# The end of a two-block network kernel: the last 256 output channels with tokens on the partitions

## The chip, the cores and the metric

The kernel runs on one core of a Trainium2 chip. The metric is the device time of one execution in microseconds, from the launch of the program to its end on the chip; the table below gives the median of three runs. A profile of one further execution gives a time for each instruction.

## What is computed

The reference runs two network blocks over 1024 tokens with 1024 channels each (attention, a state-space branch and a feed-forward part in the first; three gated branches in the second). Only the very end of the second block matters here:

```
merged = (jax.nn.sigmoid(g_a) * y_a + jax.nn.sigmoid(g_b) * y_b
          + jax.nn.sigmoid(g_c) * y_c)
return x + merged @ w_o
...
return _rmsnorm_2(x, final_g)      # x / sqrt(mean(x*x) + eps) * final_g, per token
```

`merged` is 1024 tokens by 1024 channels, `w_o` is 1024 by 1024. The mean of the norm runs over all channels of a token, so no output row can be scaled before all 1024 of its channels are known. The output is written with tokens as rows.

## The kernel before

All matrix products run with channels on the 128 partitions: an activation is held as 8 chunks of 128 channels by 1024 tokens (`act_h`, `act_l`). To keep float32 accuracy on the matmul path, each operand is split into a high and a low part, and one product is three matmuls: high x high, low x high, high x low. Weights arrive in blocks of 256 columns in `raw` (two buffers, k = 0 and 1), and GpSimd splits each block into `w_h` and `w_l` (lines 643 and 645). The results lie in PSUM, which the kernel uses as four slots of 1024 columns, two banks each (`slot(i)`).

The output product has four weight blocks (number `N_WO` to `N_WO + 3`) and so eight chunks c of 128 output channels. TensorE's code for it is a loop with two trips at lines 1314 to 1322: in each trip `product_pair` (line 746) computes two chunks interleaved into slots 2 and 3, and then `product` (through `product_half`, line 722) computes two chunks one after the other into slots 0 and 1. A chunk is 48 matmuls with 512 moving columns (tokens). Each chunk raises the semaphore `gemm`. VectorE, at line 2369, adds the chunk in PSUM to the residual in `y_t` (channels on partitions, already loaded from memory) and raises `y_ready`.

Only when all eight chunks are in `y_t` (`y_ready`) does TensorE go on to line 1328: for each of the 8 tiles of 128 tokens it makes eight 128x128 transposes into slot t % 4, which gives the tile with tokens on the partitions, and raises `otr2`. ScalarE (lines 1717, 1718) squares the 1024 columns with a running sum and takes the root of the mean (`ostd`). VectorE (lines 2374, 2377) takes the reciprocal and multiplies the tile by it and by `g_row` into one of two row buffers `o_row[:, t % 2]` (`orow`), after it has waited for the transfer of tile t - 2 out of that buffer (`row_out`). SyncE (line 621) issues the transfer of 512 KB to memory. TensorE may overwrite a slot once the tile of four before has been scaled (`orow`).

Each engine runs its own queue in the order of the code; the order between engines comes from the semaphores alone. On ScalarE and VectorE `step(...)` makes the engine wait for its own instruction before the next.

Of the kernel before, what the change touches and what calls it, by code (L numbers as in the profile page):

```python
# [7 lines left out]
ACT = mybir.ActivationFunctionType  # L8
ALU = mybir.AluOpType
# [3 lines left out]
P = 128  # L13
T = 1024
D = 1024
KD = D // P
# [37 lines left out]
def units_before(n):  # L54

    return 2 * n if n <= N_PROJ else 30 + 4 * (n - N_PROJ) if n <= N_OUT else 2 * n + 8
# [18 lines left out]
AHEAD = 3  # L75
HALF_QKV, HALF_GATE, HALF_OUT, HALF_DOWN = 0, 12, 28, 32
SQ_DOWN = 11
U_FFN, U_IN2 = 8, 24
RAISED = """gate_read qkv_read o_ready proj_read out_read down_read y_ready pv f_ready pa_read
    pb_read pc_read mb_ready mc_ready sa_ready sb_ready sc_ready pt0 sm_ready""".split()  # L80
# [42 lines left out]
def build(nc, a, out):  # L123
    ctx = ExitStack()
    with ctx:
# [3 lines left out]
        def at(name, shape, offset, dt=F32):  # L129

            return nc.alloc_sbuf_tensor_at(name, shape, dt, offset=base + offset)
# [131 lines left out]
        y_t = at("y_t", [P, KD, T], 160 * kib)  # L263
        o_row = at("o_row", [P, 2, D], 192 * kib)
        g_row = at("g_row", [P, D], 200 * kib)
        o_sq = at("o_sq", [P, D], 64 * kib)
        o_ssq = at("o_ssq", [P, 3, QB], 68 * kib)

# [59 lines left out]

        def slot(i):
            return ps[:, i, :]

        block = ctx.enter_context(nc.Block())

# [2 lines left out]
        def _(sp):  # L338
# [278 lines left out]
                load(n + 2, k, "w_o_2", (n + 2 - N_WO) * NB)  # L617

            for t in range(QB):
                sp.wait_ge(s["orow"], t + 1)  # L620
                sp.dma_start(out[0, t * P:(t + 1) * P, :], o_row[:, t % 2, :]).then_inc(row_out[t % 2], 16)
            for k in range(2):
                sp.wait_ge(row_out[k], 16 * QB // 2)
# [87 lines left out]
        def _(pe):  # L711
# [22 lines left out]
            def product_pair(slots, k, kc, high, low, ready, base=0, split=None):  # L734

                for c in range(kc):
                    if split is not None and c == 0:
                        pe.wait_ge(s["w_half"], split + 1)
                    if split is not None and c == kc // 2:
                        split_done(split)  # L740
                    pe.wait_ge(ready, base + (c + 1))
                    for cg in range(2):
                        for th in range(2):
                            tok = slice(HALF * th, HALF * th + HALF)
                            for p, (w, x) in enumerate(((w_h, high), (w_h, low), (w_l, high))):
                                last = nc.tensor.matmul(slot(slots[cg])[:, tok], w[:, k, c, P * cg:P * cg + P], x[:, c, tok],  # L746
                                                        start=(c == 0 and p == 0), stop=(c == kc - 1 and p == 2),
                                                        skip_group_check=True)
                        if c == kc - 1:
                            last.then_inc(s["gemm"], 1)  # L750
# [17 lines left out]
            def split_done(n):  # L768
                pe.wait_ge(s["w_split"], n + 1)
# [541 lines left out]


            pe.wait_ge(s["sc_ready"], AHEAD + KD)
            with pe.Fori(0, 2) as i:
                pe.wait_ge(s["y_ready"], 4 * i + (AHEAD - 2))
                split_done(2 * i + N_WO)
                product_pair((2, 3), 1, KD, act_h, act_l, s["m2_ready"])
                split_done(2 * i + N_WO + 1)
                pe.wait_ge(s["pc_read"], AHEAD + KD)
                pe.wait_ge(s["y_ready"], 4 * i + AHEAD)  # L1320
                for cg in range(2):
                    product(slot(cg), 0, cg, KD, act_h, act_l).then_inc(s["gemm"], 1)
            pe.wait_ge(s["y_ready"], AHEAD + KD)
            for t in range(QB):
                if t >= 4:
                    pe.wait_ge(s["orow"], t - 3)
                for c in range(KD):
                    last = nc.tensor.transpose(slot(t % 4)[:, P * c:P * c + P], y_t[:, c, P * t:P * t + P], ident[:])
                last.then_inc(s["otr2"], 1)


        @block.scalar
        def _(act):
# [380 lines left out]

            for t in range(QB):
                act.wait_ge(s["otr2"], t + 1)
                step(A.activation(o_sq[:], slot(t % 4), ACT.Square, accum_out=o_ssq[:, 0, t:t + 1]))
                A.activation(o_ssq[:, 1, t:t + 1], o_ssq[:, 0, t:t + 1], ACT.Sqrt, scale=1.0 / D, bias=eps_rms[:])\
                 .then_inc(s["ostd"], 1)


# [1 line left out]
        def _(dve):  # L1723
# [639 lines left out]
            for c in (KD - 2, KD - 1):  # L2363
                merged_low(c)

            for c in range(KD):
                dve.wait_ge(x2_back[c // 4], 16)
                dve.wait_ge(s["gemm"], units_before(N_WO) + c + 1)
                v.tensor_tensor(y_t[:, c, :], y_t[:, c, :], slot((c + 2) % 4), ALU.add).then_inc(s["y_ready"], 1)

            dve.wait_ge(s["g_row_in"], 16)
            for t in range(QB):
                dve.wait_ge(s["ostd"], t + 1)
                step(v.reciprocal(o_ssq[:, 2, t:t + 1], o_ssq[:, 1, t:t + 1]))
                if t >= 2:
                    dve.wait_ge(row_out[t % 2], 16 * (t // 2))
                v.scalar_tensor_tensor(o_row[:, t % 2, :], slot(t % 4), o_ssq[:, 2, t:t + 1], g_row[:],
                                       ALU.mult, ALU.mult).then_inc(s["orow"], 1)


# [13 lines left out]
```

## Time and profile before

| | us |
|---|---|
| median of 3 runs | 2178.35 |
| lowest and highest | 2176.91, 2179.33 |
| profiled execution | 2179.59 |
| its span, first to last instruction | 2177.9 |
| TensorE busy in the span | 2134.9 (98%) |
| mean granted TensorE clock | 0.992 |

The span is divided among five engines: PE is TensorE's matmuls, PEld its weight loads, DVE VectorE, ACT ScalarE, POOL GpSimd; SPq is SyncE's queue, which issues transfers. In a timeline each row has the start, the duration, engine, source line, operation, output<-inputs, shape and count, and in square brackets how long the engine had been idle before it and who released it. Matmuls overlap, so the spacing of their starts and not their duration is what one costs in a stream.

### The profile page before, as it was taken

What the parts mean: (1) busy time and instruction counts of PE and PEld (TensorE: products, weight loads), DVE (VectorE), ACT (ScalarE), POOL (GpSimd) and SP (SyncE); (2) the same over time, 40 slices, a digit from 0 to 9 for tenths busy, and PEclk for the clock granted to TensorE, in tenths of its full rate; (3) what the DMA queues carried; (4) which work ended last, traced back from release to release, by engine and by line L of the source; (5) the groups of instructions that cost most, each with busy time, mean ns of one, the idle gap of its engine ahead of it and who ended that gap; (6) DMA issues with size and microseconds to landing.
All of it is one profiled execution on the core that took longest, in us unless ns stands there. A gap on an engine that the chain in (4) does not pass through costs nothing.

```text
span 2177.9 us, 25422 instructions
## 1 busy us (share of the span) xinstructions
PE 2134.9 (98%) x10478; PEld 1777.3 (82%) x10478; DVE 789.8 (36%) x1078; ACT 406.0 (19%) x569; POOL 1046.3 (48%) x452
## 2 busy tenths in 40 slices
PE   7999999999999999999999999999999999999997
PEld 3788888888888888888888798888888888888885
DVE  6961355555553521222222665300031211331332
ACT  3302232323421310201111221111010110111102
POOL 1537446645353545445363545344554446435550
PEclk9999999999999999999999999999999999999999
DMA  9545545453451102011120231102111011101131
GB/s 347 121 103 155 194 132 154 146 174 107 169 200 51 47 24 84 29 50 48 36 71 29 69 131 54 39 29 67 59 39 49 29 58 58 49 29 58 39 125 77
DMA packets 157117, 192.26 MB, mean 88 GB/s; under 512 B 11152, under 2 KB 138720, under 8 KB 157024
## 3 DMA queue, kind: packets, MB, share of 16 engines
q1 hardware_dynamic: 148096, 172.05, 25.5%
q10 hardware_dynamic: 8928, 18.88, 2.3%
q8 instruction: 70, 1.15, 0.2%
q14 instruction: 23, 0.19, 0.0%
HBM read 159.20 MB, written 31.70 MB: 88 GB/s over the span
## 4 chain that ended last, share of the span: by engine, by line
PE 94%; DVE 2%; POOL 1%; DMA 1%; issue 0%; SPq 0%; ACT 0%; POOLq 0%; DVEq 0%; ACTq 0%
PE ps L722 64%; PE ps L798 8%; PE ps L746 8%; PE ps L1020 3%; PE ps L1189 2%; PE ps L756 2%; PE ps L981 2%; PE ps L911 1%; PE ps L995 1%; POOL w_h L643 1%; DMA ada_w<-in_w_ada 1%; PE ps L1251 1%; POOL w_l L645 1%; DVE nrm L1803 0%; PE ps L1001 0%
## 5 line engine op out<-in xcount | busy, mean ns | idle before, releaser
L643 POOL TENSOR_SCALAR w_h<-raw 128x1024 fp32r<-128x1024 f32 (+2 forms) x202 | 505.1, 2501 | 918.1 <-PE ps L722 631.3
L722 PE MATMUL ps<-act_h,w_h 128*128 128x512 f32 x1600 | 626.1, 391 | 1.2 <-POOL w_l L645 0.8
L722 PE MATMUL ps<-act_l,w_h 128*128 128x512 f32 x1600 | 623.6, 390 | 0.0
L722 PE MATMUL ps<-act_h,w_l 128*128 128x512 f32 x1600 | 623.4, 390 | 0.0
L645 POOL TENSOR_TENSOR w_l<-raw,w_h 128x1024 fp32r<-128x1024 f32 (+2 forms) x202 | 436.8, 2162 | 16.9
L722 PEld LDWEIGHTS ps<-act_h,w_h 128*128 128x128 f32 x1600 | 301.0, 188 | 67.4 <-issue 2.9
L722 PEld LDWEIGHTS ps<-act_l,w_h 128*128 128x128 f32 x1600 | 300.9, 188 | 62.7 <-issue 0.5
L722 PEld LDWEIGHTS ps<-act_h,w_l 128*128 128x128 f32 x1600 | 300.9, 188 | 62.7
L722 PE MATMUL ps<-in_h,w_h 128*128 128x512 f32 x384 | 150.6, 392 | 0.9 <-POOL w_l L645 0.9
L722 PE MATMUL ps<-in_l,w_h 128*128 128x512 f32 x384 | 149.9, 390 | 0.0
L722 PE MATMUL ps<-in_h,w_l 128*128 128x512 f32 x384 | 149.9, 390 | 0.0
L798 PE MATMUL ps<-act_h,w_h 128*128 128x512 f32 x256 | 100.3, 392 | 0.0
L798 PE MATMUL ps<-act_l,w_h 128*128 128x512 f32 x256 | 100.1, 391 | 0.0
L798 PE MATMUL ps<-act_h,w_l 128*128 128x512 f32 x256 | 100.1, 391 | 0.0
L746 PE MATMUL ps<-act_h,w_h 128*128 128x512 f32 x224 | 88.7, 396 | 5.6 <-DVE act_l L1814 4.5
L2115 DVE SCALAR_TENSOR_TENSOR conv<-ps,cols_b,conv 128x1023 f32<-128x1023 f32 (+1 forms) x32 | 40.8, 1281 | 141.0 <-ACT conv L1576 139.1
L746 PE MATMUL ps<-act_l,w_h 128*128 128x512 f32 x224 | 88.2, 394 | 0.0
L746 PE MATMUL ps<-act_h,w_l 128*128 128x512 f32 x224 | 88.1, 393 | 0.0
L722 PEld LDWEIGHTS ps<-in_h,w_h 128*128 128x128 f32 x384 | 72.5, 189 | 16.5 <-POOL w_l L645 1.3
L722 PEld LDWEIGHTS ps<-in_l,w_h 128*128 128x128 f32 x384 | 72.4, 189 | 15.3 <-issue 0.2
L2274 DVE TENSOR_TENSOR br<-br,ps 128x1024 f32<-128x1024 f32 x14 | 17.1, 1221 | 186.7 <-PE ps L722 186.7
L722 PEld LDWEIGHTS ps<-in_h,w_l 128*128 128x128 f32 x384 | 72.4, 188 | 15.0
(339 smaller groups left out, 2739.9 us busy)
## 6 DMA issues: line engine op xcount, KB each, us to landing
raw<-in_w_in SPq DMA_DIRECT2D x45, 1024.0 KB, 5.3
raw<-in_w_up SPq DMA_DIRECT2D x16, 1024.0 KB, 5.4
ada_w<-in_w_ada SPq DMA_DIRECT2D x8, 1024.0 KB, 12.0
ada_lo<-in_w_ada SPq DMA_DIRECT2D x16, 512.0 KB, 3.8
ada_hi<-in_w_ada SPq DMA_DIRECT2D x16, 512.0 KB, 4.8
gates_scratch<-gate_st ACTq DMA_DIRECT2D x32, 256.0 KB, 2.2
gate_in<-gates_scratch SPq DMA_DIRECT2D x16, 512.0 KB, 4.6
raw<-in_w_down SPq DMA_DIRECT2D x16, 512.0 KB, 3.5
```

The costliest lines, as they stand in the source:

```text
L643: nc.gpsimd.tensor_scalar(w_h[:, k, c, :], src[:, c, :], 1.0, None, ALU.mult).then_inc(s["w_high"], 1)
L645: nc.gpsimd.tensor_tensor(w_l[:, k, c, :], src[:, c, :], w_h[:, k, c, :].bitcast(F32), ALU.subtract).then_inc(done, 1)
L722: last = nc.tensor.matmul(dst[:, tok], w[:, k, kw + c, P * cg:P * cg + P], x[:, c, tok], start=(c == 0 and p == 0), stop=(c == kc - 1 and ...
L746: last = nc.tensor.matmul(slot(slots[cg])[:, tok], w[:, k, c, P * cg:P * cg + P], x[:, c, tok], start=(c == 0 and p == 0), stop=(c == kc - ...
L756: last = nc.tensor.matmul(dst[:, NB * t:NB * t + NB], x[:, c, tok], w[:, k, c, :], start=(c == 0 and p == 0), stop=(c == KD - 1 and p == 2 ...
L798: last = nc.tensor.matmul(slot(1)[:, HALF:T], w[:, n % 2, c, P * (j % 2):P * (j % 2) + P], x[:, c, tok], start=(c == 0 and p == 0), stop=( ...
L911: last = nc.tensor.matmul(dst, c_act[:, c:c + 1], ada_w[:, 2 * i:2 * i + 2, c, :], start=(c == 0), stop=(c == KD - 1))
L981: last = nc.tensor.matmul(slot(t % 2)[:, c0:c0 + w], q2[:, e, P * qb:P * qb + P], k[:, e, c0:c0 + w], start=(k is k_hh), stop=(k is k_ll))
L995: last = nc.tensor.transpose(slot(2)[:, P * b:P * b + P], src[:, P * b:P * b + P], ident[:])
L1020: last = nc.tensor.matmul(dst[:, 0:HD], src[:, P * b:P * b + P], v_st[:, pair % 2, b, HD * (h % 2):HD * (h % 2) + HD], start=(b == 0), sto ...
L1189: last = nc.tensor.matmul(rows_of(h, b, t), x[:, c, tok], w[:, 1 - b, c, :], start=(c == 0 and p == 0), stop=(c == KD - 1 and p == 2), ski ...
L2115: ins = v.scalar_tensor_tensor(conv[:, cg, j:T], slot(cg)[:, 0:T - j], cols_b[:, bass.ds(4 * q + (at_b["w_conv"] + j * (FF // P) + c), 1)] ...
```

## The change

The last weight block (output channels 768 to 1023) is no longer computed with channels on the partitions. For each tile of 128 tokens, `last_columns(t)` makes 24 matmuls with the activation tile as the stationary operand and the 256 weight columns as the moving one, so the result has tokens on the partitions; it goes to one bank of slot 2. `to_rows(t)` transposes the tile: six transposes of chunks 0 to 5 of `y_t` into slot t % 2, and two of chunks 6 and 7, which hold only the residual, into one bank of slot 3. The order on TensorE is last_columns(0), to_rows(0), and so on up to tile 6, then to_rows(7), last_columns(7). Chunks 4 and 5 are computed by `product`, one after the other, and the loop is written out.

ScalarE squares 768 columns out of PSUM, scales the sum and adds eps with an `Identity`, waits for VectorE, squares the other 256 columns out of `o_row`, and takes the root with the first result as bias. VectorE copies the residual's 256 columns from slot 3 to `o_row`, adds slot 2 to them, and then scales the 256 and the 768 columns with two instructions. The scratch `o_sq` moves, since `w_h` is still in use.

```diff
@@ TensorE
-            with pe.Fori(0, 2) as i:
-                pe.wait_ge(s["y_ready"], 4 * i + (AHEAD - 2))
...
-            pe.wait_ge(s["y_ready"], AHEAD + KD)
-            for t in range(QB):
-                if t >= 4:
-                    pe.wait_ge(s["orow"], t - 3)
                 for c in range(KD):
-                    last = nc.tensor.transpose(slot(t % 4)[:, P * c:P * c + P], y_t[:, c, P * t:P * t + P], ident[:])
+            split_done(N_WO + 2)
+            for cg in range(2):
+                pe.wait_ge(s["y_ready"], AHEAD + cg + 1)
+                product(slot(2 + cg), 1, cg, KD, act_h, act_l).then_inc(s["gemm"], 1)
+
+            def last_columns(t):
+
+                pe.wait_ge(s["y_ready"], AHEAD + (5 if t < 2 else LAST_C + t - 1))
+                for c in range(KD):
+                    tok = slice(t * P, (t + 1) * P)
+                    for p, (w, x) in enumerate(((w_h, act_h), (w_h, act_l), (w_l, act_h))):
+                        last = nc.tensor.matmul(last_of(0, t), x[:, c, tok], w[:, 0, c, :],
+                                                start=(c == 0 and p == 0), stop=(c == KD - 1 and p == 2))
+                last.then_inc(s["gemm"], 1)
+
+            def to_rows(t):
+
+                if t == 0:
+                    pe.wait_ge(s["y_ready"], AHEAD + LAST_C)
+                    pe.wait_ge(x2_back[1], 16)
+                if t >= 2:
+                    pe.wait_ge(s["orow"], 2 * (t - 1))
+                for c in range(KD):
+                    dst = slot(t % 2)[:, P * c:P * c + P] if c < LAST_C else last_of(1, t)[:, P * (c - LAST_C):P * (c - LAST_C) + P]
+                    last = nc.tensor.transpose(dst, y_t[:, c, P * t:P * t + P], ident[:])
                 last.then_inc(s["otr2"], 1)
+
+            split_done(N_WO + 3)
+            for t in range(QB - 1):
+                last_columns(t)
+                to_rows(t)
+            to_rows(QB - 1)
+            last_columns(QB - 1)
@@ ScalarE
-                step(A.activation(o_sq[:], slot(t % 4), ACT.Square, accum_out=o_ssq[:, 0, t:t + 1]))
-                A.activation(o_ssq[:, 1, t:t + 1], o_ssq[:, 0, t:t + 1], ACT.Sqrt, scale=1.0 / D, bias=eps_rms[:])\
+                step(A.activation(o_sq[:], slot(t % 2)[:, 0:LAST_C * P], ACT.Square, accum_out=o_ssq[:, 0, t:t + 1]))
+                step(A.activation(o_ssq[:, 1, t:t + 1], o_ssq[:, 0, t:t + 1], ACT.Identity, scale=1.0 / D, bias=eps_rms[:]))
+                act.wait_ge(s["y_ready"], AHEAD + LAST_C + t + 1)
+                step(A.activation(o_sq[:, 0:NB], o_row[:, t % 2, LAST_C * P:D], ACT.Square, accum_out=o_ssq[:, 2, t:t + 1]))
+                A.activation(o_ssq[:, 3, t:t + 1], o_ssq[:, 2, t:t + 1], ACT.Sqrt, scale=1.0 / D, bias=o_ssq[:, 1, t:t + 1])\
                  .then_inc(s["ostd"], 1)
@@ VectorE
             for t in range(QB):
-                dve.wait_ge(s["ostd"], t + 1)
-                step(v.reciprocal(o_ssq[:, 2, t:t + 1], o_ssq[:, 1, t:t + 1]))
+                most, rest = slice(0, LAST_C * P), slice(LAST_C * P, D)
+                row = o_row[:, t % 2, :]
                 if t >= 2:
                     dve.wait_ge(row_out[t % 2], 16 * (t // 2))
-                v.scalar_tensor_tensor(o_row[:, t % 2, :], slot(t % 4), o_ssq[:, 2, t:t + 1], g_row[:],
+                dve.wait_ge(s["otr2"], t + 1)
+                step(v.tensor_copy(row[:, rest], last_of(1, t)))
+                dve.wait_ge(s["gemm"], units_before(N_WO) + LAST_C + t + 1)
+                v.tensor_tensor(row[:, rest], row[:, rest], last_of(0, t), ALU.add).then_inc(s["y_ready"], 1)
+                dve.wait_ge(s["ostd"], t + 1)
+                step(v.reciprocal(o_ssq[:, 4, t:t + 1], o_ssq[:, 3, t:t + 1]))
+                v.scalar_tensor_tensor(row[:, rest], row[:, rest], o_ssq[:, 4, t:t + 1], g_row[:, rest],
+                                       ALU.mult, ALU.mult).then_inc(s["orow"], 1)
+                v.scalar_tensor_tensor(row[:, most], slot(t % 2)[:, most], o_ssq[:, 4, t:t + 1], g_row[:, most],
                                        ALU.mult, ALU.mult).then_inc(s["orow"], 1)
```

`LAST_C` is 6; `last_of(m, t)` is the first 256 columns of bank t % 2 of slot 2 + m. SyncE's wait for a row becomes `2 * t + 2`, since VectorE now raises `orow` twice for each tile.

## Rows read from the trace of the kernel before

**Rows 1.** The page: busy time of each engine, and the chain's shares by engine.
```profile
PE 2134.9 (98%) x10478; PEld 1777.3 (82%) x10478; DVE 789.8 (36%) x1078; ACT 406.0 (19%) x569; POOL 1046.3 (48%) x452
PE 94%; DVE 2%; POOL 1%; DMA 1%; issue 0%; SPq 0%; ACT 0%; POOLq 0%; DVEq 0%; ACTq 0%
```
**Rows 2.** The chain that ended last, 2050 to 2178: start, duration, what.
```profile
2132.56 21.77 PE ps L722 x96
...
2161.17 2.69 DMA out<-o_row
```
**Rows 3.** Timeline of the tail, 2119 to 2178 us.
```profile
2119.08 2.40 POOL L645 TENSOR_TENSOR w_l<-raw,w_h 128x1024 fp32r<-128x1024 f32 x1
...
2154.43 1.22 DVE L2369 TENSOR_TENSOR y_t<-y_t,ps 128x1024 f32<-128x1024 f32 x1 [9.66 <-PE ps L722]
2155.70 3.71 PE L1328 MATMUL ps<-ident,y_t 128*128 128x128 f32 x32 [1.39 <-DVE y_t L2369]
...
2157.97 1.28 ACT L1718 ACT_TABLE_LOAD   x1
...
2159.46 1.00 ACT L1717 ACTIVATE o_sq<-ps 128x1024 f32<-128x1024 f32 x1
...
2159.85 1.28 DVE L2377 SCALAR_TENSOR_TENSOR o_row<-ps,o_ssq,g_row 128x1024 f32<-128x1024 f32 x1
...
2160.59 0.29 ACT L1718 ACTIVATE o_ssq<-o_ssq,eps_rms 128x1 f32<-128x1 f32 x1
...
2163.95 1.28 DVE L2377 SCALAR_TENSOR_TENSOR o_row<-ps,o_ssq,g_row 128x1024 f32<-128x1024 f32 x1 [1.35 <-DMA out<-o_row]
...
2173.46 1.28 DVE L2377 SCALAR_TENSOR_TENSOR o_row<-ps,o_ssq,g_row 128x1024 f32<-128x1024 f32 x1
```
**Rows 4.** Timeline: first and last matmul of the last block's 96.
```profile
2132.40 0.39 PE L722 MATMUL ps<-act_h,w_h 128*128 128x512 f32 x1
...
2153.93 0.39 PE L722 MATMUL ps<-act_h,w_l 128*128 128x512 f32 x1
```
**Rows 5.** Line 1189: its summary (min/median/max ns, starts) and four rows of its timeline.
```profile
L1189 PE MATMUL ps<-w_h,act_h x128: 280/283/679, 1253.2 to 1304.7; 128*128 128x256 f32 x128
...
1253.23 0.55 PE L1189 MATMUL ps<-w_h,act_h 128*128 128x256 f32 x1 [2.86 <-DVE acc L2155]
...
1255.93 0.41 PE L1189 MATMUL ps<-w_h,act_h 128*128 128x256 f32 x1
...
1287.88 0.28 PE L1189 MATMUL ps<-w_h,act_l 128*128 128x256 f32 x1
...
1304.08 0.28 PE L1189 MATMUL ps<-w_h,act_l 128*128 128x256 f32 x1
```
**Rows 6.** Timeline: eight transposes at line 1241 between products.
```profile
1315.95 1.03 PE L1241 MATMUL ps<-ident,ws_tok 128*128 128x128 f32 x8
...
1317.06 0.40 PE L722 MATMUL ps<-act_l,w_h 128*128 128x512 f32 x1
```
**Rows 7.** Groups by shape: operations with 256 columns; busy us, mean ns.
```profile
L1998 DVE SCALAR_TENSOR_TENSOR ada_part<-ada_lo,c_act,ada_part 128x256 f32<-128x256 f32 x48 | 28.2, 588 | 1.1
...
L1891 DVE COPY ct<-ps 64x256 f32<-64x256 f32 x2 | 0.8, 422 | 0.1
...
L1480 ACT ACTIVATE pt_short<-ps 128x256 f32<-128x256 f32 x8 | 3.1, 384 | 20.4 <-PE ps L995 20.4
```
**Rows 8.** Windows: busy us (count) of each engine, then granted clock, DMA share, GB/s.
```profile
500.00:600.00 100.00, 99.32 (x558) 85.84 (x557) 58.82 (x110) 36.58 (x57) 38.62 (x19) 1.00 0.43 146
...
2156.00:2162.00 6.00, 4.22 (x39) 3.98 (x38) 2.27 (x4) 5.07 (x10) 0.00 (x0) 1.00 0.00 1
```
**Rows 9.** ScalarE's timeline, 1225 to 1262 us: a root and an `Identity`.
```profile
1240.32 0.30 ACT L1604 ACTIVATE stat<-stat,eps_sq 128x4 f32<-128x4 f32 x1 [1.44 <-DVE stat L2174]
...
1247.68 1.26 ACT L1372 ACTIVATE act_h<-ps 128x512 fp32r<-128x512 f32 x2 [2.21 <-DVE ps L1803]
```
**Rows 10.** The chain again, 1210 to 1230: the longest pause without a cause.
```profile
1221.78 1.17 issue
```

More of the change, by code:

```diff
@@ L77 @@
 SQ_DOWN = 11
+LAST_C = 6
 U_FFN, U_IN2 = 8, 24
@@ L265, in build @@
         g_row = at("g_row", [P, D], 200 * kib)
-        o_sq = at("o_sq", [P, D], 64 * kib)
-        o_ssq = at("o_ssq", [P, 3, QB], 68 * kib)
+        o_sq = at("o_sq", [P, LAST_C * P], 96 * kib)
+        o_ssq = at("o_ssq", [P, 5, QB], 104 * kib)
         tiles = [(h, qb) for h in range(HEADS) for long in range(QB - 1, QB // 2 - 1, -1) for qb in (long, QB - 1 - long)]
@@ L332, in slot, with last_of @@
             return ps[:, i, :]
+        def last_of(m, t):
+            return slot(2 + m)[:, HALF * (t % 2):HALF * (t % 2) + NB]
         block = ctx.enter_context(nc.Block())
@@ L619, in _ @@
             for t in range(QB):
-                sp.wait_ge(s["orow"], t + 1)
+                sp.wait_ge(s["orow"], 2 * t + 2)
                 sp.dma_start(out[0, t * P:(t + 1) * P, :], o_row[:, t % 2, :]).then_inc(row_out[t % 2], 16)
@@ L1313, in _ @@
             pe.wait_ge(s["sc_ready"], AHEAD + KD)
-            with pe.Fori(0, 2) as i:
-                pe.wait_ge(s["y_ready"], 4 * i + (AHEAD - 2))
[L1316 to L1322, printed above, removed]
@@ L1323, in _ @@
-            pe.wait_ge(s["y_ready"], AHEAD + KD)
-            for t in range(QB):
-                if t >= 4:
-                    pe.wait_ge(s["orow"], t - 3)
-                for c in range(KD):
-                    last = nc.tensor.transpose(slot(t % 4)[:, P * c:P * c + P], y_t[:, c, P * t:P * t + P], ident[:])
-                last.then_inc(s["otr2"], 1)
+            pe.wait_ge(s["y_ready"], AHEAD - 2)
+            split_done(N_WO)
+            product_pair((2, 3), 1, KD, act_h, act_l, s["m2_ready"])
@@ new lines, in _ @@
+            split_done(N_WO + 1)
+            pe.wait_ge(s["pc_read"], AHEAD + KD)
+            for cg in range(2):
+                product(slot(cg), 0, cg, KD, act_h, act_l).then_inc(s["gemm"], 1)
+            split_done(N_WO + 2)
+            for cg in range(2):
+                pe.wait_ge(s["y_ready"], AHEAD + cg + 1)
+                product(slot(2 + cg), 1, cg, KD, act_h, act_l).then_inc(s["gemm"], 1)
+            def last_columns(t):
+                pe.wait_ge(s["y_ready"], AHEAD + (5 if t < 2 else LAST_C + t - 1))
+                for c in range(KD):
+                    tok = slice(t * P, (t + 1) * P)
[3 more added lines that the diff above has]
+                last.then_inc(s["gemm"], 1)
@@ L2364, in _ @@
                 merged_low(c)
-            for c in range(KD):
+            for c in range(LAST_C):
                 dve.wait_ge(x2_back[c // 4], 16)
```

## The prediction

> **What bounds the kernel now.** I read the page first: TensorE is busy for 98% of the span and holds 94% of the chain that ended last, so in general only TensorE work shortens this kernel [rows 1]. The diff touches the end alone, so I then read the chain of waits there. It runs through TensorE without a gap to 2154.33 us (the last block of 96 matmuls is one piece of 21.77 us), and from there to the end of the span at 2177.9 it is on other things [rows 2]. Those last 23.57 us are what the change can win. The timeline shows what they hold [rows 3]: VectorE adds the last chunk to `y_t`, TensorE transposes, ScalarE squares (1.00), loads a table (1.28) and takes the root, and at 2159.85 VectorE writes the first output row. Then eight rows leave through two buffers: VectorE waits for the landing of an older row (1.35 us at 2163.95, three such waits), and a 512 KB row takes 2.69 us [rows 2, 3]. The last row is computed by 2174.74 and 3.16 us later the span ends. So the end is a serial ping-pong of four engines that begins only when the products are done.
>
> **Where the new block starts.** The two loop trips are written out; chunks 0 to 5 keep their matmul counts. Chunks 4 and 5 change from interleaved to one after the other, so chunk 4 is free for VectorE 10.88 us sooner and only chunk 5's add (1.22 us, the duration of the row at 2154.43 [rows 3]) follows at 2132.6. The first matmul of the last block waits for chunk 4's add, which is then long done, and for the weight split, whose last step of the whole kernel is over at 2121.48 [rows 3]. The block starts at 2132.40 as before [rows 4]. The first transposes wait for chunk 5's add (2133.9) and come at 2135.3: covered by the first tile's products. I cost these edits at nothing; if that cover were gone, 1.4 us, the gap before the transposes now [rows 3].
>
> **Products of the last block.** Before: 96 matmuls with 512 columns, first to last start 21.53 us for 95 steps, 0.2266 each, 21.76 in all [rows 4]. After: 192 with 256 columns, `act` stationary and `w` moving. The kernel already has this very form at line 1189: 135 steps in 16.20 us, 0.120 each [rows 5]. 192 x 0.120 = 23.04, so +1.28 us. Bounds: half of a 512 step (0.1133) gives 21.75, so 0; the whole group at line 1189, 384 (128 of each operand pair) from 1253.2 to 1304.7 with a low clock at its start and other matmuls between, gives 0.134, so 25.8 and +4.0 [rows 5]. I take 0.120: the steady stretch of the same form, at full clock like the block that it replaces. For a half-width matmul the Trainium skill (TensorE: Matmul & The Clock Gate, Back-to-back issue gap) has 256/2.4 + 2.5 = 109 ns for an isolated gap; the sum by that would be 2.1 us lower, and the row of 0.120 disagrees.
>
> **Transposes on TensorE.** 64 remain. Put between products they cost what line 1241 shows: eight begin at 1315.95 and last 1.03, and the second product behind them starts at 1317.06; one step of 0.227 would lie between the start of their place and that second product without them, so eight cost 1.11 - 0.23 = 0.88 us [rows 6]. Tiles 0 to 5 stand alone (6 x 0.88); tiles 6 and 7 stand together: 0.88 + 8 x 0.11 = 1.77, from 32 transposes in 3.71 us [rows 3]. Sum 7.05. TensorE is through with its steps at 2132.40 + 23.04 + 7.05 = 2162.49; the last matmul lasts 0.28 and not 0.12 [rows 5], so its end is at 2162.65, which is 8.32 us later than the 2154.33 of now.
>
> **The chain of one tile.** Does the rest keep up with TensorE's period of 24 x 0.120 + 0.88 = 3.76 us? Count from the end E of the tile's last transpose. ScalarE: square of 768 columns 0.92 (a 1024-column one holds the engine 1.13 to the next operation, rows at 2159.46 and 2160.59 [rows 3], less 256 columns at 0.82 ns), identity on one column 0.29 (by the root's row): E + 1.24. VectorE meanwhile: copy of 256 columns 0.45 with its own wait [rows 7], add of 256 columns 0.42 (1.22 less 768 columns at 1.04 ns), E + 0.95. Then the square of 256 columns 0.52 (0.38 by a 256-column activation [rows 7], and the accumulator read as with the large one), root 0.29, hand-over 0.11, reciprocal 0.19 up to the multiply, multiply of 256 columns 0.40, multiply of 768 columns 1.02 (1.28 for 1024 at 1.04 ns a column [rows 3, 7]): E + 3.77, and VectorE can begin the next tile at E + 3.69. That is just below 3.76. Row transfers of 2.69 us in two buffers need 3.77 + 2.8 = 6.6 us for two tiles of 7.5: the landing waits go. Tile 0 also holds the table load (1.28) and is 1.2 us late; a late VectorE finds ScalarE's large square already done, so its period is then 3.4 and the lateness is worked off by tile 4.
> Who waits for whom anew: behind VectorE's wait for the row buffer now stands the copy, and behind that the add for which the products of tile t + 2 wait; those come a period later, so with 3 us of cover. `to_rows(7)` comes right after tile 6's and needs both multiplies of tile 5: up to 0.3 us stall, hidden since VectorE is later anyway. SyncE's queue holds nothing else at that time; its eight waits change only their count.
>
> **The new end.** E of tile 6 is 2132.40 + 7 x 2.88 + 6 x 0.88 + 1.03 = 2158.87. VectorE is free at 2162.56, copies tile 7 to 2163.01 and adds to 2163.43, so it is 0.3 us behind TensorE. Then 0.06 + 0.52 + 0.29 + 0.11 + 0.19 + 0.40 + 1.02 = 2.59: the last row is computed at 2166.0. With the same 3.16 behind it the span ends at 2169.2. So the sum is: last row's end 2174.74 to 2166.0, -8.7 us. As a ledger: products +1.28, transposes +7.05, last matmul's shape -0.01, and what follows TensorE shrinks from 23.57 to 6.55, -17.02.
>
> **Clock.** The sum takes full clock. The granted clock is 1.00 from 2156 to 2162 us, where TensorE only transposes, and from 500 to 600, where transposes stand among products [rows 8]; that is the 2.4 GHz level. The Trainium skill (TensorE: Matmul & The Clock Gate, PE-mode transpose) says that transposes do not count as TensorE work for the clock in the way matmuls do, which speaks against putting them between products. By the rows at full clock the sum stays; by that rule it would become the second rival's.
>
> **Rivals.**
> 1. *The VectorE and ScalarE chain becomes the bound.* It is within 0.1 us of TensorE's period, made of ten steps and six hand-overs; the 256-column multiply has only rows taken under other load (0.59 [rows 7]). From 3.76 us on every excess counts eight times. At 4.3 us a tile: 2136.31 + 8 x 4.3 + 3.16 = 2173.9 in the span, 2174.3 in the median's terms. It would give all back at (2174.74 - 2136.31) / 8 = 4.8 us.
> 2. *Slower: the clock falls in the last block.* From 1253.23 to 1255.93 the same matmul takes 2.70 us for 13 steps, 0.208 each [rows 5]; that is the 1.2 GHz level, behind an idle of 2.86 us. At that the products cost 192 x 0.088 = 16.9 more: 2186.5. It decides from 99 of the 192 matmuls at the low level. For: the clock does fall where TensorE pauses. Against: there is no idle ahead of this block, and the rows 8.
> 3. *Table flips.* If the new `Identity` and the root did not share a table, each tile would load two, 1.28 each; a chain of 4.7 us gives about 2177. Against: from 1225 to 1262 `Square`, `Sqrt` (line 1604) and `Identity` (line 1372) alternate with no load between them [rows 9].
> 4. *It doesn't do what it says.* The straight code must be fetched, and TensorE pauses for it: one unexplained pause of 1.17 us stands in the chain at 1221.78 [rows 10]. Two of them: 2171.9.
>
> **How the numbers follow.** The profiled execution took 2179.59, of which 1.69 lie outside the span; the median shown is 2178.35. I take the 8.7 off the median: 2169.6 (off the profiled one: 2170.9, span 2169.2). Chances: forecast with rival 4's small pauses 0.80; chain bound with a gain under 0.2% 0.09; table flips 0.03; clock 0.05; another loss that I don't see 0.03. Below, the sum reaches 2166.8: matmuls at half of a 512 step (-1.3), VectorE not late (-0.3), and 1.2 for the spread of the runs. Above I take rival 1 at 4.3 us a tile: 2174.5. About 0.2%, 4.4 us, is what a measurement of this kernel can tell from no change: faster 0.80, within 0.12, slower 0.08.
>
> **What would show it.** Right: 192 matmuls of 256 columns at 0.12, no TensorE idle over 0.3 us until about 2162.7, no VectorE wait for an `out` landing, last row computed 3.4 us after the last matmul, clock 1.00. Wrong: VectorE's tiles spaced over 3.8 us with TensorE waiting in `last_columns` or `to_rows` for `y_ready` or `orow`; steps of 0.21 us; a table load per tile.

## The result and the profile after

| | before | after |
|---|---|---|
| median, us | 2179.35 | 2168.92 |
| lowest and highest of 6 runs each | 2176.91, 2179.91 | 2167.01, 2171.76 |
| span of the profiled execution | 2177.9 | 2166.8 |
| granted TensorE clock, mean | 0.992 | 0.994 |

The ratio after / before is 0.9956, with a 95% interval from 0.9943 to 0.9969: faster by 0.44%, more than the 0.2% that a measurement of this kernel can tell. Two more comparisons of the same pair gave 0.9964 [0.9953, 0.9976] and 0.9964 [0.9951, 0.9976]. The forecast was 2169.6.

The chain of waits of after, from 2126 us on (start, duration, what), shows the new order:

```profile
2130.33 2.87 PE ps L1337 x24
2133.20 0.87 PE ps L1350 x8
2134.07 2.87 PE ps L1337 x24
...
2152.77 2.87 PE ps L1337 x24
2155.64 0.89 PE ps L1350 x8
...
2156.55 0.91 ACT o_sq L1746 x2
...
2159.28 1.01 DVE o_row L2417
2160.30 0.34 DVE o_row L2410
...
2160.68 0.43 DVE o_row L2412
...
2161.19 0.52 ACT o_sq L1749 x2
```

Line 1337 is `last_columns`, line 1350 `to_rows`. Seven times 24 products and eight transposes follow each other in one unbroken line: a tile costs TensorE 2.87 + 0.87 = 3.74 us. Where the chain of before left TensorE at 2154.33 for 23.57 us [rows 2], this one leaves it at tile 6's transposes, at 2156.53, since VectorE and ScalarE are a little behind it from there on.

VectorE's timeline, 2134 to 2167 us, shows the cadence of the rows. Line 2417 is the multiply of 768 columns, 2410 the residual's copy, 2412 the add of the products, 2415 the multiply of 256 columns:

```profile
2134.18 0.42 DVE L2410 COPY o_row<-ps 128x256 f32<-128x256 f32 x1 [2.52 <-PE ps L1350]
...
2138.12 1.01 DVE L2417 SCALAR_TENSOR_TENSOR o_row<-ps,o_ssq,g_row 128x768 f32<-128x768 f32 x1
...
2141.48 1.01 DVE L2417 SCALAR_TENSOR_TENSOR o_row<-ps,o_ssq,g_row 128x768 f32<-128x768 f32 x1
...
2155.54 1.01 DVE L2417 SCALAR_TENSOR_TENSOR o_row<-ps,o_ssq,g_row 128x768 f32<-128x768 f32 x1
...
2159.28 1.01 DVE L2417 SCALAR_TENSOR_TENSOR o_row<-ps,o_ssq,g_row 128x768 f32<-128x768 f32 x1
...
2160.68 0.42 DVE L2412 TENSOR_TENSOR o_row<-o_row,ps 128x256 f32<-128x256 f32 x1
...
2162.66 1.01 DVE L2417 SCALAR_TENSOR_TENSOR o_row<-ps,o_ssq,g_row 128x768 f32<-128x768 f32 x1
```

The eight multiplies are 3.36 us apart three times, then 3.59, 3.74, 3.74 and, for the last, 3.38. That is the late VectorE that catches up and from then on follows TensorE's 3.74. The last row is computed at 2163.67 and the span ends 3.13 later. Three of the waits in the stretch from 2126 us on: of VectorE for ScalarE's root, of ScalarE's second square for VectorE's add, and the only one of TensorE (us in total, times, longest):

```profile
DVE o_ssq L2414 <- ACT o_ssq L1750: 9.9, 8, 2.5
...
ACT o_sq L1749 <- DVE o_row L2412: 3.1, 4, 1.4
...
PEld ps L1350 <- DVE o_row L2417: 0.3, 1, 0.3
```

VectorE no longer waits for the landing of an `out` row; before, it did so three times [rows 3]. TensorE has the one stall of 0.3 us in `to_rows(7)`.

One thing has to be taken apart before the spans are compared. The last block starts at 2132.40 before [rows 4] and at 2130.17 after, though nothing ahead of it differs in cost. So 2.2 of the 11.1 us between the spans aren't the change's (the last section shows where they come from). What I compare below is the *distance*: from the first matmul of the last block to the end of the span. It is 2177.9 - 2132.40 = 45.5 us before and 2166.8 - 2130.17 = 36.6 after, so the change wins 8.9 us. This distance repeats: three profiled executions of after give 36.63, 36.60 and 36.63. Before was profiled once, but the kernel of the first experiment, whose end is the same as before's, gives 45.5 too.

### The profile page after: what moved, and what is told of

It reads as the page before. It is cut to its first block, busy times and chain, and to the rows that moved or that the text cites. A ratio compares the mean times of both kernels' runs of the same rounds, so it can differ in the third digit from the quotient of the medians.

```text
span 2166.8 us, 25663 instructions
## 1 busy us (share of the span) xinstructions
PE 2133.2 (98%) x10574; PEld 1780.7 (82%) x10574; DVE 790.8 (36%) x1100; ACT 411.1 (19%) x593; POOL 1047.5 (48%) x452
## 4 chain that ended last, share of the span: by engine, by line
PE 95%; DVE 2%; POOL 1%; DMA 1%; issue 0%; SPq 0%; ACT 0%; DVEq 0%; POOLq 0%; ACTq 0%
PE ps L727 64%; PE ps L803 8%; PE ps L751 7%; PE ps L1025 3%; PE ps L1194 2%; PE ps L761 2%; PE ps L986 2%; PE ps L916 1%; PE ps L1000 1%; PE ps L1337 1%; POOL w_h L648 1%; DMA ada_w<-in_w_ada 1%; PE ps L1256 1%; POOL w_l L650 1%; DVE acc L2187 0%
## 5 line engine op out<-in xcount | busy, mean ns | idle before, releaser
L727 PE MATMUL ps<-act_h,w_h 128*128 128x512 f32 x1600 | 625.8, 391 | 0.9 <-POOL w_l L650 0.5
L727 PE MATMUL ps<-act_l,w_h 128*128 128x512 f32 x1600 | 623.1, 389 | 0.0
L727 PE MATMUL ps<-act_h,w_l 128*128 128x512 f32 x1600 | 623.1, 389 | 0.0
L803 PE MATMUL ps<-act_h,w_h 128*128 128x512 f32 x256 | 100.3, 392 | 0.0
L803 PE MATMUL ps<-act_l,w_h 128*128 128x512 f32 x256 | 100.1, 391 | 0.0
L803 PE MATMUL ps<-act_h,w_l 128*128 128x512 f32 x256 | 100.1, 391 | 0.0
L751 PE MATMUL ps<-act_h,w_h 128*128 128x512 f32 x192 | 76.4, 398 | 5.9 <-DVE act_l L1846 4.5
L673 POOL TENSOR_SCALAR k_hh<-q 128x1024 fp32r<-128x1024 f32 x8 | 22.2, 2775 | 119.5 <-DMA k_ll<-qk_scratch 119.5
L751 PE MATMUL ps<-act_l,w_h 128*128 128x512 f32 x192 | 75.8, 395 | 0.0
```

The lines of the kernel that those rows point to most:

```text
L673: stage_step(nc.gpsimd.tensor_scalar(k_hh[:, e, :], q.bitcast(F32), 1.0, None, ALU.mult))
L727: last = nc.tensor.matmul(dst[:, tok], w[:, k, kw + c, P * cg:P * cg + P], x[:, c, tok], start=(c == 0 and p == 0), stop=(c == kc - 1 and ...
L803: last = nc.tensor.matmul(slot(1)[:, HALF:T], w[:, n % 2, c, P * (j % 2):P * (j % 2) + P], x[:, c, tok], start=(c == 0 and p == 0), stop=( ...
```

## Experiments

My theory: the edit wins because the chain of seven small steps per tile now runs while TensorE multiplies, and it loses nothing as long as a tile's chain stays under TensorE's 3.74 us. Rivals: part of the gain comes from the written-out loop with chunks 4 and 5 one after the other; the token form is good by itself and the transposes' place between the products doesn't matter; the gain is really that of the row buffers' landing waits, which could be had more cheaply. Each distance is to be read against 45.5 and 36.6.

**The written-out loop alone.** The kernel before, with TensorE's loop written out and chunks 4 and 5 by `product`; the end as before.

```diff
-            with pe.Fori(0, 2) as i:
...
+            split_done(N_WO + 2)
+            for cg in range(2):
+                pe.wait_ge(s["y_ready"], AHEAD + cg + 1)
+                product(slot(2 + cg), 1, cg, KD, act_h, act_l).then_inc(s["gemm"], 1)
```

> The kernel before with one part of the change alone: the loop of the output product is written out and chunks 4 and 5 are computed one after the other. My theory (the gain is made behind the start of the last block, and the 2 us by which the profiled execution of the changed kernel reaches that block sooner are scatter between executions): no difference, ratio 0.999 to 1.001; the last block starts 65.4 us after the output product's first matmul, as before. Rival (part of the gain belongs to this edit, since the changed kernel's profile is 2.1 us ahead at the start of the last block): 1.5 to 2.5 us faster, ratio 0.9990 to 0.9988 at the least, and a shorter distance from the first matmul of the output product to the last block.

Measured: 2179.71 us, ratio 1.0005 [0.9996, 1.0015]; span 2175.8, block from 2130.30, distance 45.5. From the first matmul of the output product (2064.93) to the last block are 65.4 us, as before (2066.96 to 2132.40). The edit costs and brings nothing, as the prediction had it; the first rival falls. The kernel after ran on the same chip beside it:

> The changed kernel itself, unedited, beside the others on this chip. Theory: ratio 0.9960 (8.7 us); from the first matmul of the last block to the end of the span 36.5 us where the kernel before has 45.5, whatever the stages ahead of it do. Rival (the gain includes 2 us of stages ahead): the distance from the last block to the end differs by more than 0.3 us from 36.5, or the start of the last block lies 2 us ahead of the kernel before again.

It gave 2169.18 us, ratio 0.9964, distance 36.6. The last block starts at 2132.50 in its profile, level with before; the 2.2 us of the first profile of after were not the change's.

**Token form, but nothing between the products.** The kernel after with all 192 products first; VectorE moves each tile's result to a buffer of its own meanwhile.

```diff
-            for t in range(QB - 1):
-                last_columns(t)
-                to_rows(t)
-            to_rows(QB - 1)
-            last_columns(QB - 1)
+            for t in range(QB):
+                last_columns(t)
+            for t in range(QB):
+                to_rows(t)
@@ VectorE, ahead of its rows
+            for t in range(QB):
+                dve.wait_ge(s["gemm"], units_before(N_WO) + LAST_C + t + 1)
+                v.tensor_copy(tail[:, t, :], last_of(0, t)).then_inc(s["y_ready"], 1)
```

> The changed kernel, with the last 256 channels still computed with tokens on the partitions, but all eight tiles' products first and all transposes and the norm behind them; VectorE copies each tile's products to a scratch tile in between, and adds the residual later. Theory (the form of the matmul itself costs 1.3 us, all of the gain is that the norm and the rows run under products): products 23.1, first transposes 1.0, tile 0 5.0 with the table load, then 7 tiles at about 2.95 (add 0.48, square 0.52, root 0.29, hand-over 0.11, reciprocal 0.19, multiplies 1.33), last row to the end 3.1: 52.9 us from the start of the last block to the end of the span, so 7.4 slower than before (45.5), 2186.8. Rival (the gain comes from the token form itself, from no chunk having to be complete for all tokens, or from the smaller square and multiply): still faster than before, under 2178.

Measured: 2187.05 us, ratio 1.0042 [1.0028, 1.0055], distance 52.5: 7 us worse than before. Its chain and VectorE's timeline behind the products:

```profile
2132.95 23.03 PE ps L1338 x192
```

```profile
2160.90 1.01 DVE L2420 SCALAR_TENSOR_TENSOR o_row<-ps,o_ssq,g_row 128x768 f32<-128x768 f32 x1
...
2163.80 1.01 DVE L2420 SCALAR_TENSOR_TENSOR o_row<-ps,o_ssq,g_row 128x768 f32<-128x768 f32 x1
...
2181.21 1.01 DVE L2420 SCALAR_TENSOR_TENSOR o_row<-ps,o_ssq,g_row 128x768 f32<-128x768 f32 x1
```

The 192 products take 23.03 us (192 x 0.120), 1.3 more than the 96 of before, and behind them the rows come 2.90 us apart: 20.3 us from the first multiply to the last, against 13.6 before, landing waits included (2159.85 to 2173.46 [rows 3]). So the token form is by itself a loss on both counts: more matmul time and a longer chain per row. The interleaving is worth 52.5 - 36.6 = 15.9 us, and the whole gain is its work. The second rival falls.

This kernel differs from after in two more things: each tile's eight transposes now follow VectorE's multiplies, since there are two slots, and they take longer.

```profile
2164.87 1.97 PE L1351 MATMUL ps<-ident,y_t 128*128 128x128 f32 x8 [0.94 <-DVE o_row L2420]
```

and in before:

```profile
2165.28 1.09 PE L1328 MATMUL ps<-ident,y_t 128*128 128x128 f32 x8 [1.61 <-DVE o_row L2377]
```

Both stand behind a wait, but these take 1.97 us and before's 1.09: the granted clock is 0.50 there, the 1.2 GHz level (the section on why the prediction was right shows the windows). Neither sets the pace of the rows. The second row's transposes were done at 2157.7, long ahead, and its multiply comes 2.90 us after the first one's, as far as all later ones.

Not tried was an overlap without the token form: a chunk's product runs through the first 512 tokens and then through the other 512, so with the two chunks of the last block ordered by token halves the first four tiles could go out under the second half's products. How much of the gain that would have is open.

**Four row buffers in the kernel before.** This takes the landing waits away, by what makes them, and leaves the rest.

```diff
-        o_row = at("o_row", [P, 2, D], 192 * kib)
+        o_row = at("o_row", [P, 4, D], 96 * kib)
...
-                if t >= 2:
-                    dve.wait_ge(row_out[t % 2], 16 * (t // 2))
+                if t >= 4:
+                    dve.wait_ge(row_out[t % 4], 16 * (t // 4))
```

> The kernel before with four row buffers in place of two, nothing else: the output rows no longer wait for an older row to land. Theory (the 23.6 us behind the products are mostly a serial chain, of which the landing waits of 4.0 us in the profile are only a part): VectorE's eight multiplies follow at 1.39 each from 2159.85 to about 2171, unless the transposes with four slots hold them; 3.5 us faster, ratio 0.9984, last row computed 8 x 1.39 + 5.5 = 16.6 us behind the last product in place of 20.4. Rival (what the change gains is the landing waits going, so this cheaper edit gets most of it): 7 us or more, ratio 0.9968 or below. Third possibility: the transfers themselves are the bound (8 of 512 KB at 1.3 us each under full load), then also about 3 us.

Measured: 2175.19 us, ratio 0.9986 [0.9976, 0.9995], distance 41.6. VectorE's timeline:

```profile
2154.76 1.28 DVE L2377 SCALAR_TENSOR_TENSOR o_row<-ps,o_ssq,g_row 128x1024 f32<-128x1024 f32 x1
...
2164.48 1.28 DVE L2377 SCALAR_TENSOR_TENSOR o_row<-ps,o_ssq,g_row 128x1024 f32<-128x1024 f32 x1
```

From the first multiply to the eighth are 9.72 us, 1.39 from one to the next and without a gap; the landing waits are gone and 3.9 us with them. That is 0.44 of what the change wins (3.9 of 8.9), for a handful of lines. The transfers themselves were not the bound: from the last row's end (2165.76) to the end of the span are 3.1 us, as in before. The other 5.0 need the overlap: even at VectorE's full pace the eight rows and their lead-in stand behind the last product.

**The order of the last two tiles.** `to_rows(7)` behind `last_columns(7)`, as for all other tiles.

```diff
-            for t in range(QB - 1):
+            for t in range(QB):
                 last_columns(t)
                 to_rows(t)
-            to_rows(QB - 1)
-            last_columns(QB - 1)
```

> The changed kernel with the order of the last two pieces of TensorE's work exchanged: the products of tile 7 come before its transposes, as with all other tiles. Theory (from the last transpose of a tile to its finished row are 3.74 us in the changed kernel's profile, from the last product of tile 7 only 3.1, because its large square and its copy are done by then): the last row is finished 0.6 us later; from the last block's first matmul to the end of the span 37.1 us where the changed kernel has 36.5. Rival (the place of the last transposes makes no difference, TensorE does the same work in both): 36.5.

Measured: 2167.8 us, ratio 0.9946 [0.9926, 0.9965], distance 36.98 and so 0.35 more than after's 36.63. The medians can't tell the two; the distance can. It comes near the 37.1 that was expected, but the step is 0.35 where 0.6 was expected. The last row is done 3.75 us behind TensorE's end where after has 3.10, since the transposes stand behind the last product and ScalarE's large square behind those; and TensorE ends 0.29 us sooner, since the stall of 0.3 us in `to_rows(7)` is not in this kernel's waits. The expectation had left that out.

**Where the chain becomes the bound.** The residual's copy is made twice, and four times, with the same result each time; so the chain of one tile is longer by one and by three copies of 0.46 us.

```diff
-                step(v.tensor_copy(row[:, rest], last_of(1, t)))
+                for _ in range(2):
+                    step(v.tensor_copy(row[:, rest], last_of(1, t)))
```

> The changed kernel with VectorE's copy of the residual's 256 columns made twice for each tile, 0.46 us more in its chain. Theory (a late VectorE needs 3.36 us a tile, TensorE 3.74, so the cover is 0.4 us a tile and this edit just uses it up; the lateness of tile 0 by the table load is then no longer worked off): VectorE's tiles are spaced 3.82, the last row is finished 2.3 us later, 38.8 us from the last block's start to the end in place of 36.5. Rival (TensorE is the bound with room to spare): at most 0.5 us later, 37.0.

Measured: 2172.23 us, ratio 0.9974 [0.9962, 0.9985], distance 39.8, 1.0 more than expected. The multiplies stand 3.82 us apart, as expected, but once 4.57; VectorE's timeline there, and the chain:

```profile
2151.75 0.88 DVE L2411 COPY o_row<-ps 128x256 f32<-128x256 f32 x2 [0.66 <-DMA out<-o_row]
```

```profile
2147.30 4.42 DMA out<-o_row
```

A row took 4.42 us to land where the others take 2.7, and the buffer wait came back for once. I had not expected that; the last section returns to it. It makes 0.75 of the 1.0 us (4.57 for 3.82). The other 0.2 stand in tile 0: its large multiply starts 8.19 us after the block (2138.62 - 2130.43), in after 7.95 (2138.12 - 2130.17), which the expectation had left out.

> The changed kernel with the same copy made four times for each tile, 1.37 us more. Theory (the chain of VectorE and ScalarE becomes the bound; my prediction put the point at which all of the gain is gone at 4.8 us a tile): tiles spaced 4.73 us, last row finished 9.5 us later, 46.0 us from the last block's start to the end, where the kernel before has 45.3: no gain left, ratio 1.000. TensorE then waits in the last block. Rival (only the last tile's chain counts, each added copy costs once): 1.4 us later, 37.9.

Measured: 2180.29 us, ratio 1.0009 [0.9998, 1.002], distance 46.4 (46.0 expected). The multiplies are 4.73 us apart, and now TensorE waits for VectorE's add, as the prediction said that a chain-bound kernel would show it:

```profile
PE ps L1337 <- DVE o_row L2413: 3.1, 4, 1.0
```

TensorE also waits 3.3 us in `to_rows(7)`. So a tile of 4.73 us gives back all 8.9 us and 0.9 more. Going back from there by 0.9 / 8 = 0.11, the break-even lies at about 4.6 us a tile, where the prediction worked out 4.8. After's tiles follow each other in 3.74 us, about 0.9 below it.

One row of this kernel was as slow to land as that of the copy-twice kernel, 4.5 us. Nothing waited for it: with 4.73 us a tile the buffer isn't needed sooner.

**Half as much in the token form.** Only the last 128 channels with tokens on the partitions; chunk 6 goes as the others. That is 192 matmuls of 128 columns, and VectorE's and ScalarE's small steps are shorter.

```diff
-LAST_C = 6
+LAST_C = 7
+LB = 128
...
+            pe.wait_ge(s["y_ready"], AHEAD + 3)
+            product(slot(0), 0, 0, KD, act_h, act_l).then_inc(s["gemm"], 1)
             for t in range(QB - 1):
```

> The changed kernel with one size changed: only the last 128 channels are computed with tokens on the partitions (192 matmuls with 128 moving columns), chunk 6 as the ones before it (48 with 512). Theory (a step of a matmul with 128 columns can't be shorter than that of the 128-column transposes, 0.11): chunk 6 10.9 us, 192 x 0.11 = 21.1, transposes 7.05; TensorE needs 39.0 us in place of 30.1, and the end comes 45.4 us after the last block's start: as slow as before. Rival (the step follows the columns, 0.06 at 128): 192 x 0.06 = 11.5, 29.4 us on TensorE, and the VectorE chain takes over at 3.0 to 3.4 us a tile: 45.4 is not reached, about 42 (chunk 6 10.9, then eight tiles at 3.4 and 4).

Measured: 2176.82 us, ratio 0.9996 [0.9985, 1.0008]; 46.7 us from chunk 6's first matmul to the end (45.4 expected). Its chain, and VectorE's timeline:

```profile
2143.66 2.63 PE ps L1338 x24
...
2168.64 4.48 DMA out<-o_row
```

```profile
2173.14 0.29 DVE L2413 COPY o_row<-ps 128x128 f32<-128x128 f32 x1 [1.00 <-DMA out<-o_row]
```

24 matmuls of 128 columns take 2.63 us, 0.110 each, against 0.120 for twice the columns: below 256 columns a matmul of this kind hardly gets cheaper, so half the channels cost nearly as much TensorE time and the gain is gone. Of the 1.3 us above the expectation up to 1.00 is again a landing wait, behind a row of 4.48 us. (An earlier row of 3.2 us made a wait of 0.22, which was worked off.)

**The last row in three pieces, and four buffers.** In both, the last row leaves as its 256 columns first and then two times 384, each as soon as it is scaled; the second also has four row buffers.

```diff
+            for k, (a0, b0) in enumerate(((LAST_C * P, D), (0, 3 * P), (3 * P, LAST_C * P))):
+                sp.wait_ge(s["orow"], 2 * QB - 1 + k)
+                sp.dma_start(out[0, (QB - 1) * P:QB * P, a0:b0], o_row[:, 1, a0:b0]).then_inc(row_out[1], 16)
...
+                for part in ((most,) if t < QB - 1 else (slice(0, 3 * P), slice(3 * P, LAST_C * P))):
```

> The changed kernel; tile 7's row leaves in three pieces (256, 384, 384 columns) as VectorE finishes them, its large multiply being split into two. Theory (the 3.1 us behind the last multiply are part fixed and part the bytes of a 512 KB row): two thirds of the bytes are under way sooner, the multiply's split costs 0.1; 36.2 us from the last block's first matmul to the end in place of 36.6. Rival (the 3.1 us are all fixed cost of a transfer): 36.7.

> The same and four row buffers in place of two. Theory (in the copy-twice run and the 128-channel run one row took 4.4 us to land in place of 2.7 and VectorE waited for it; in the changed kernel itself such a row would have cover, so the buffers bring nothing in the common case): 36.2 again, ratio to the kernel before 0.9959, same as the changed kernel within what a measurement can tell. Rival (slow landings cost the changed kernel some of its runs): 1 us less than the changed kernel's 2169.0, ratio 0.9952.

> The changed kernel unedited, on the same chip as the two above. Theory: 36.6 us from the last block's first matmul to the end, ratio 0.9960.

Measured: 2168.32 us, ratio 0.9952 [0.9935, 0.997], distance 36.03 for the pieces; 2168.92, 0.9954 [0.9937, 0.9971], 36.09 with four buffers besides; after itself 2171.55, 0.9964 [0.9951, 0.9976], 36.63. The pieces win 0.6 us in the distance, 0.03%, which the medians can't tell. The four buffers add nothing where no landing wait stands. Whether they would help in an execution with a 4.4 us row was not seen: the profiled one had none.

## Why the prediction was right

- *Where the block starts, written-out loop.* Cost nothing: ratio 1.0005 and the same distance in the first experiment. The absolute start of 2132.40 did not hold (2130.17), for a reason that has nothing to do with the change. It makes up 2.2 of the 2.4 us by which the span (2166.8, predicted 2169.2) came out lower.
- *Products, 192 x 0.120 = 23.04.* Held: 23.03 in one piece in the third experiment, 2.87 for 24 in after. The steady stretch of the same form at line 1189 [rows 5] was the right row, better than half of a 512-column step.
- *Transposes, 0.88 for eight.* Held at 0.87. After's PE timeline shows both kinds of place:

```profile
2151.74 1.04 PE L1350 MATMUL ps<-ident,y_t 128*128 128x128 f32 x8
...
2155.48 2.23 PE L1350 MATMUL ps<-ident,y_t 128*128 128x128 f32 x16
```

  Sixteen in a row take 2.23 us. They were costed at 1.77 as steps; with the end of the last one, which the eight alone show to be 1.04 - 0.87 = 0.17, that is 1.94, and the other 0.3 are the stall in `to_rows(7)`. The prediction named this stall with that size, but called it hidden. Its TensorE end was 30.25 us behind the block's start; it came at 30.40 (2160.57).
- *The chain of one tile.* E + 3.77 predicted; E of tile 6 is 2156.53 and its row is done at 2160.29, 3.76. The late period was 3.36 (3.4 predicted), the lateness was worked off by tile 4, and there was one table load of 1.28 us, at tile 0. The terms agree to a hundredth or two: from the multiply of 256 columns to the next start 0.40 (it lasts 0.48, but the two overlap), the square of 768 with its accumulator read 0.91, that of 256 0.52.
- *The new end.* VectorE was predicted 0.3 us behind TensorE and was 0.1: the stall had made TensorE later and not VectorE. From the last product's end to the last row 3.1 (3.3 predicted, 2162.65 to 2166.0), then 3.13 to the end (3.16). Behind TensorE stand 6.23 us where 6.55 were predicted.
- *The ledger.* TensorE ends 30.40 instead of 21.93 us behind the start of the block: +8.47 (+8.32 predicted). Behind it 23.57 shrink to 6.23: -17.34 (-17.02). Sum -8.87, where -8.7 was predicted.
- *Clock.* Full, as taken from [rows 8]. After's windows (us, busy (count) of PE, PEld, DVE, ACT, POOL, then granted clock, DMA share, GB/s):

```profile
2130.00:2140.00 10.00, 10.00 (x86) 9.96 (x85) 4.40 (x8) 4.48 (x10) 0.00 (x0) 1.00 0.01 2
2140.00:2150.00 10.00, 10.00 (x88) 10.00 (x87) 6.98 (x15) 5.71 (x17) 0.00 (x0) 1.00 0.39 159
2150.00:2160.00 10.00, 9.90 (x85) 9.67 (x85) 6.15 (x14) 6.19 (x19) 0.00 (x0) 1.00 0.39 157
2160.00:2167.00 7.00, 0.57 (x5) 0.37 (x4) 2.62 (x6) 0.80 (x3) 0.00 (x0) 0.88 0.37 150
```

  The granted clock is 1.00, the 2.4 GHz level, as long as TensorE works, with transposes making 0.87 of every 3.74 us. The Trainium skill (TensorE: Matmul & The Clock Gate, PE-mode transpose) says that a transpose does not count as TensorE work for the clock in the way a matmul does; in this mixture that did not become a cost, and the trace gives no reason to fear a low clock from it. Two kernels show longer stretches of transposes alone. In before they run, with pauses of 0.3 to 1.8 us, from 2155.70 to 2167.76, and the clock stays at 1.00 throughout. In the kernel with nothing between the products TensorE stood idle from 2157.7 to 2161.97, and then only transposes ran until 2178.4. Its windows:

```profile
2159.00:2161.00 2.00, 0.00 (x0) 0.00 (x0) 0.67 (x3) 1.99 (x4) 0.00 (x0) 1.00 0.00 0
2162.00:2164.00 2.00, 1.93 (x8) 1.53 (x8) 1.00 (x4) 0.84 (x4) 0.00 (x0) 0.50 0.62 252
2170.00:2178.00 8.00, 5.47 (x23) 4.67 (x24) 5.00 (x12) 5.77 (x18) 0.00 (x0) 0.50 0.42 169
```

  The clock fell in the pause, and transposes for 1.97 of every 2.90 us did not bring it back. The products at line 1189, without a gap, did: their steps are 0.208 us up to 1255.93 and 0.12 from 1256.30 on. So a high clock was held by transposes, a low one was not raised; whether that lies in the transposes or in the pauses of 0.94 us between them no run separates.
- *Rivals.* The chain-bound case did not come, and the experiment with four copies shows the mechanism. Its price was put too low: the sum for rival 1, and with it the break-even of 4.8 us, leaves out tile 0's table load, which a chain-bound kernel can't work off. With it the break-even is (2174.74 - 2136.31 - 1.28) / 8 = 4.6, which is what the four copies gave; 4.3 us a tile would then have ended at about 2175.6 in the median's terms, above the stated range. No table flips (one load in the tail), no pauses between products. Rival 4 read its row wrongly: the 1.17 us at 1221.78 [rows 10] lie inside VectorE's work, whose multiply at 1221.74 lasts 1.28, and TensorE's matmuls go on there every 0.23 us. Of a pause of TensorE for code that row says nothing.

Where the sum was luckier than it was sound: it left 0.9 us a pair of tiles for the landing waits (6.6 of 7.5), on transfers of 2.7 us. Three of the experiments had a row of 4.4 to 4.5 us. In after's three profiled executions no such row fell; the prediction gave it no chance of its own. An estimate from after's times: tile 5's row lands at 2159.2, 1.0 us before tile 7 needs its buffer (2160.21), so 1.8 us more would cost 0.8 there; for the last row, behind which nothing is left to do, they would cost the whole 1.8.

The median, too, is closer than the sum could promise: 2168.92 for 2169.6. The medians of the three comparisons lie 10.4, 8.6 and 6.2 us apart, and the forecast started from one of 2178.35 where six executions gave 2179.35. What the prediction got right is the distance, -8.87 for -8.7.

## What to carry to other kernels

When a serial chain of small steps stands behind the last product, give the last block the layout that the chain needs, even if its matmuls cost more, and put each tile's chain under the next tile's products; here the layout without the interleaving was a loss of 7 us, with it a gain of 8.9. Work out the period of the chain against the period of the engine that covers it, tile by tile, and look at the first tile (table load) and the last two by themselves. Try the cheap remedy (more buffers) alone as well: here it had 0.44 of the gain.

## What the runs showed of the hardware

**The same code takes different times through the granted clock, far from the change.** The last block started anywhere from 2127.3 to 2133.1 us in these executions. The windows from 100 to 170 us of before, of after, and of after's third profiled execution, in this order (columns as above):

```profile
100.00:170.00 70.00, 70.00 (x461) 59.65 (x460) 41.28 (x33) 9.30 (x15) 28.31 (x10) 0.95 0.56 110
```

```profile
100.00:170.00 70.00, 70.00 (x467) 59.63 (x466) 42.06 (x34) 10.18 (x15) 30.39 (x11) 0.98 0.56 114
```

```profile
100.00:170.00 70.00, 70.00 (x475) 59.71 (x474) 41.41 (x32) 9.64 (x14) 32.08 (x12) 1.00 0.55 114
```

TensorE is busy for the whole of it in all three and gets through 461, 467 and 475 matmuls: more at the higher granted clock. Blocks started at 2132.4, 2130.2 and 2127.8 in this order. Most of the difference is made here: line 1189's matmuls (1194 in after) start at 1253.23, 1250.79 and 1248.47. From 1222 to 1257 us the clock differs too (0.90, 0.95 and 0.95), but that adds little: the kernel with the written-out loop alone has 0.98 in the first stretch and 0.90 in the second, and starts line 1189 at 1250.98, 0.2 us behind after. The clock of these stretches follows the execution and not the kernel: after's second profiled execution had 0.95 in the first and 0.90 in the second, as before had, and started its block at 2132.50. What decides it was not found. It is why 5 us between two spans of this kernel prove nothing, and a distance inside the span does.

**A 512 KB row can take 4.4 to 4.5 us to land instead of 2.7** (2.69 [rows 2]; 4.42, 4.5 and 4.48 in the copy-twice, the copy-four-times and the 128-channel kernels), at the same size. The transfers of the copy-twice kernel from 2147 to 2153 us, in 40 slices of 0.15 us, with the queues (packets, MB, share of the engines' time):

```profile
GB/s 0 0 0 0 0 0 0 246 382 437 437 355 410 328 437 355 137 0 0 0 0 0 27 0 0 27 0 27 0 0 0 0 0 410 437 410 437 410 410 410
...
q8 instruction: 1, 0.02, 1.0%
```

Nearly all of the row moves in the usual 1.5 us, up to 2149.6. A packet of 16 KB on the instruction queue starts at 2149.48 (109 of the 137 GB/s in its slice) and takes 0.93 us. At 2150.40, when it is over, three single 4 KB packets of the row follow, in slices of 27 GB/s (27 x 0.15 = 4 KB each), the last at 2151.11, and only then has the row landed. The copy-four-times kernel from 2152 to 2158 us shows the same order, the instruction packet at 2154.59 and the row's late ones from 2155.51 on:

```profile
GB/s 0 0 0 0 0 0 218 410 437 382 410 355 382 382 410 55 0 109 0 0 0 0 0 27 0 0 27 0 0 0 0 0 0 0 0 0 0 0 410 410
```

In the 128-channel kernel the packet runs from 2169.69 to 2171.15, and the row's late packets start at 2171.15. The three profiled executions of after, the plain-order kernel and both kernels with the row in pieces have such a packet in the tail too, but it starts at or behind the last 4 KB packet of a row, and that row lands in 2.65 to 2.74 us. It fits that the piece of the row on one of the 16 DMA engines queued behind an instruction fetch, and that it is chance whether a fetch meets a row. This is argued from three cases and from their times, and not shown: no run moved the fetch.

**Narrow matmuls stop getting cheaper.** In steady streams at full clock one step took 0.2266 us with 512 columns [rows 4], 0.120 with 256 (192 in 23.03 us) and 0.110 with 128 (24 in 2.63 us). From 512 to 256 columns a column's cost stays nearly the same; from 256 to 128 it nearly doubles.
